# The two left-over rows of each expert: half of their gate and up products moved from TensorE to VectorE

## The chip, the cores and the metric

The kernel runs on one core of a Trainium2 chip. The metric is device time in microseconds (us) of one execution; the median of three runs before the change was 2638.13 us. A core has TensorE (PE in the profile; its weight loads are PEld), VectorE (DVE), ScalarE (ACT), GpSimd (POOL) and SyncE (SP, which here only issues transfers), and 16 DMA engines that move data between memory (HBM) and the on-chip SBUF. TensorE writes its sums into PSUM.

## The reference, cut to what matters

Two transformer blocks run one after the other on 512 tokens of width 1024. The change lies in the last stage, the mixture of experts of the second block. Each of 16 experts takes the 66 of 528 tokens that score best for it (2 x 528 / 16), and computes on them

```
hg = einsum('becd,edf->becf', xg, w_gate)      # 66 x 1024 by 1024 x 2048
hu = einsum('becd,edf->becf', xg, w_up)        # 66 x 1024 by 1024 x 2048
y  = einsum('becf,efd->becd', silu(hg) * hu, w_down)   # 66 x 2048 by 2048 x 1024
y  = y * top_aff[..., None]
```

and adds the rows to the tokens that they came from. All of it is float32. One expert's three matrices are 25.2 MB, and each is used for 66 rows only.

## The kernel before

**The expert stage** is the last 40% of the program. Tokens are the stationary operand and weights are streamed through TensorE. The array is used in four quarters of 32 columns: `four` issues four matmuls of 128x32 by 128x512, one for each quarter, which run side by side. 64 of the 66 rows fill two quarters, so one `four` multiplies them with 2 x 512 columns of weights. The two left-over rows (`LEFT` = 2) take a `four` of their own, in which each quarter holds the same two rows and takes another 512 columns.

**The order on TensorE** (`expert`). The gate and up products are made in two halves h of 1024 columns each. A half has 8 steps k over the 1024 inputs, and each step has three `four`s: gate, up (the 64 rows), and left-over. Both halves make 48 `four`s. `turn_hidden` transposes the products of the 64 rows and of the left-over rows back into stationary form, in the midst of the second half for h = 0 and within the down stage for h = 1. The down product is 24 `four`s: in four pieces (h, b) of 4 for the 64 rows and 2 for the left-over rows. That is 72 `four`s for an expert. `turn_x` transposes the next expert's gathered tokens before the last piece.

**The weights** come in 12 loads of 2 MB for each expert (0 to 3 gate and up of the first half, 4 to 7 of the second, 8 to 11 down), into a ring of 8 slots (`expert_ring_low`, `expert_ring_high`). SyncE issues them strictly in order (`pair_loads`, `load_read`): load n waits until the slot of load n - 8 has been read, which TensorE tells by the counts `w_used`, `left_summed` and `down_left_summed`.

**The other engines.** ScalarE takes the silu of the gate sums and copies transposed data. VectorE multiplies with the up sums, copies, scales the next tokens (`take_x`) and, once the down sums are complete, the output rows (`YM` for 64 rows in two halves, `YL` for the left-over ones). GpSimd gathers the tokens of the expert after the next (`gather`) and adds the output rows to memory (`scatter`), by indirect transfers. Before the stage, ScalarE writes the tokens' rows to memory in 12 transfers out of the four buffers `TMS`; GpSimd's second gather waits for all 12 (`rows_out`).

The two SyncE lines on which a step of the prediction rests:

```
                if j in (3, 7):
                    sp.wait_ge(S("left_summed"), pair * 16 + 8 * r + (4 if j == 3 else 8))
```

## Time and profile before

| | |
|---|---|
| median of 3 runs | 2638.13 us (2638.09 to 2641.3) |
| the profiled execution, its own time | 2637.16 us |
| its span, first to last instruction | 2635.4 us |
| PE, DVE, ACT, POOL busy over the span | 95%, 42%, 31%, 14% |
| mean granted TensorE clock | 0.978 of full speed |
| the expert stage's matmuls, L1135 | 9216 records, 509.7 + 504.8 us busy |
| the 192 loads of expert weights | 2048 KB each, median 11.4 us from issue to landing |

Each float32 matmul of the program leaves two records in the trace, so a `four` is eight. GB/s is what all transfers of the core moved. A wait is written as: who waited, for whom, how long in total.

### The profile page before, as it was taken

How to read it: one execution, taken by the hardware profiler on the slowest of the kernel's cores; microseconds unless marked ns; L12 is line 12 of the kernel's file. 1: busy time of each engine (PE TensorE's matmuls, PEld its weight loads, DVE VectorE, ACT ScalarE, POOL GpSimd, SP SyncE). 2: the span in 40 equal slices, each digit the busy share in tenths (PEclk: the TensorE clock that was granted, in tenths of full speed). 3: DMA queues.
4: the chain of work that ended last, by engine and by line, in shares of the span. 5: the costliest groups of instructions: out<-in, count | busy, mean ns of one | idle time of the engine just before them, and what ended most of it. 6: DMA issues, size and time to landing. Idle time of an engine off the chain costs nothing.

```text
span 2635.4 us, 42597 instructions
## 1 busy us (share of the span) xinstructions
PE 2514.9 (95%) x18335; PEld 1566.6 (59%) x18335; DVE 1097.4 (42%) x1506; ACT 821.0 (31%) x1361; POOL 374.0 (14%) x423
## 2 busy tenths in 40 slices
PE   8998899999989999999989979999999999999996
PEld 6755468887779898989889953333333333333332
DVE  4335456664538898987574541111111111111111
ACT  3255544443344545554545230000000000000001
POOL 0024012111102212123421200000000000000000
PEclk9999999999989999999989989999999999999998
DMA  5100068888845454646524549999999999999993
GB/s 206 71 32 1 32 239 289 290 281 283 276 158 192 150 196 136 201 145 217 146 96 162 212 153 408 400 398 401 395 400 398 396 395 395 395 397 401 396 406 120
DMA packets 129718, 676.36 MB, mean 257 GB/s; under 512 B 19300, under 2 KB 52068, under 8 KB 100228
## 3 DMA queue, kind: packets, MB, share of 16 engines
q1 hardware_dynamic: 56624, 554.81, 54.1%
q0 software_dynamic: 25632, 88.49, 10.0%
q10 hardware_dynamic: 47284, 30.42, 4.3%
q8 instruction: 145, 2.38, 0.4%
q14 instruction: 33, 0.27, 0.0%
HBM read 618.55 MB, written 55.12 MB: 256 GB/s over the span
## 4 chain that ended last, share of the span: by engine, by line
PE 79%; DVE 8%; DMA 6%; ACT 4%; issue 2%; POOL 1%; ACTq 0%; POOLq 0%; DVEq 0%
PE PS L1135 38%; PE PS L825 11%; PE PS L1007 4%; PE PS L771 3%; PE PS L767 3%; DMA arena<-w_proj 3%; PE PS L768 3%; PE PS L1012 2%; DMA ring<-ssd_sums 2%; ACT ring L1509 2%; PE PS L671 1%; PE PS L622 1%; PE PS L618 1%; PE PS L619 1%; PE PS L742 1%
## 5 line engine op out<-in xcount | busy, mean ns | idle before, releaser
L1135 PE MATMUL PS<-expert_ring_low,U 128*32 128x512 f32 x4608 | 509.7, 594 | 0.9 <-DVE U L2264 0.9
L1135 PE MATMUL PS<-expert_ring_high,U 128*32 128x512 f32 x4608 | 504.8, 592 | 0.0
L825 PE MATMUL PS<-XH,RINGF 128*128 128x264 f32 x2304 | 393.9, 289 | 1.2 <-ACT arena L1453 1.2
L1135 PEld LDWEIGHTS PS<-expert_ring_high,U 128*32 128x32 f32 x4608 | 148.0, 110 | 336.9 <-issue 335.9
L1135 PEld LDWEIGHTS PS<-expert_ring_low,U 128*32 128x32 f32 x4608 | 146.2, 110 | 332.8 <-issue 331.7
L825 PEld LDWEIGHTS PS<-XH,RINGF 128*128 128x128 f32 x2304 | 325.6, 190 | 9.1 <-issue 6.8
L825 PE MATMUL PS<-UH,RINGF 128*128 128x264 f32 x1152 | 234.8, 286 | 0.0
L2276 DVE TENSOR_TENSOR H<-H,PS 128x512 f32<-128x512 f32 x32 | 22.0, 688 | 439.3 <-PE PS L1135 423.8
L2016 DVE SCALAR_TENSOR_TENSOR H<-arena,par,H 128x528 f32<-128x528 f32 x240 | 187.1, 823 | 1.3
L825 PEld LDWEIGHTS PS<-UH,RINGF 128*128 128x128 f32 x1152 | 180.7, 191 | 0.0
L1712 ACT ACTIVATE H<-PS 128x512 f32<-128x512 f32 x32 | 19.1, 598 | 457.8 <-PE PS L1135 457.8
L2465 POOL DMA_INDIRECT residual_rows<-H,scatter_rows x16 | 25.1, 1572 | 930.8 <-DVE H L2290 930.8
L767 PE MATMUL PS<-UX,WF 128*128 128x512 f32 x352 | 138.5, 393 | 1.0 <-DVE UX L1758 1.0
L768 PE MATMUL PS<-UX,WF 128*128 128x512 f32 x352 | 137.1, 389 | 0.0
L1896 DVE TENSOR_TENSOR PREL<-arena,PS 128x1024 fp32r<-128x1024 f32 x66 | 80.5, 1220 | 119.6 <-ACT PS L1360 119.4
L2067 DVE SCALAR_TENSOR_TENSOR SQ<-arena,par,SQ 128x528 f32<-128x528 f32 x144 | 109.7, 766 | 6.4 <-ACT SQ L1441 3.7
L1360 ACT ACTIVATE PS<-arena 128x1024 fp32r<-128x1024 f32 x66 | 67.8, 1027 | 142.8 <-DMA arena<-w_proj 141.1
L2371 POOL TENSOR_TENSOR arena<-arena,ring 128x512 f32<-128x512 f32 (+1 forms) x32 | 60.2, 1886 | 318.4 <-ACT arena L1534 258.7
L1723 ACT ACTIVATE SQ<-PS 2x512 f32<-2x512 f32 x32 | 18.9, 591 | 260.6 <-PE PS L1135 260.2
L1509 ACT ACTIVATE ring<-ring 128x128 f32<-128x128 f32 (+1 forms) x320 | 89.3, 368 | 17.9 <-issue 12.0
L2282 DVE COPY U<-PS 128x256 f32<-128x256 f32 x32 | 13.6, 425 | 191.1 <-PE PS L1129 191.1
L1344 ACT ACTIVATE WF<-ring 128x1024 fp32r<-128x1024 f32 (+1 forms) x76 | 71.3, 940 | 59.8 <-PE PS L771 59.6
(350 smaller groups left out, 3695.6 us busy)
## 6 DMA issues: line engine op xcount, KB each, us to landing
expert_ring_low<-w_experts SPq DMA_DIRECT2D x96, 2048.0 KB, 11.4
expert_ring_high<-w_experts SPq DMA_DIRECT2D x96, 2048.0 KB, 11.4
arena<-w_proj POOLq DMA_DIRECT2D x72, 512.0 KB, 5.0
projection_low_parts<-PREL POOLq DMA_DIRECT2D x72, 512.0 KB, 5.0
ring<-w_proj SPq DMA_DIRECT2D x72, 512.0 KB, 3.7
RINGF<-projection_low_parts SPq DMA_DIRECT2D x72, 512.0 KB, 4.7
ring<-w_gu SPq DMA_DIRECT2D x11, 2048.0 KB, 9.3
ring<-ssd_sums ACTq DMA_DIRECT2D x32, 512.0 KB, 8.4
```

The lines of the kernel that those rows point to most:

```text
L767: nc.tensor.matmul(PS[:, bank, :], hi[:, k, :], src[:, 0, k0 + k, :], start=(start and k == 0), stop=False)
L768: nc.tensor.matmul(PS[:, bank, :], hi[:, k, :], src[:, 1, k0 + k, :], start=False, stop=False)
L771: last = nc.tensor.matmul(PS[:, bank, :], lo[:, k, :], src[:, 0, k0 + k, :], start=False, stop=(stop and k == n - 1))
L825: last = nc.tensor.matmul(PS[:, banks[i], 0:HT], w[:, k, :], x[:, k, lo:hi], start=start, stop=stop)
L1007: nc.tensor.matmul(PS[:, banks[i], 0:HT], wh[:, k, :], x(k)[:, lo:hi], start=(first and k == 0 and x is high), stop=False)
L1135: mm = nc.tensor.matmul(PS[QUAD * t:QUAD * t + QUAD, bank, :], stat(t), move(t), start=start, stop=stop)
L1344: A(split_high(p), raw(p), ACT.Copy).then_inc(S("weights_high"), 1)
L1360: A(pre_high_place(q), pre_raw(q), ACT.Copy).then_inc(S("pre_high"), 1)
L1509: ins = A(FR[i % 2][d][0:n, h, 0:n], FR[i % 2][d][0:n, h, 0:n], ACT.Exp, bias=FT[0:n, c, j:j + 1])
L1896: V_.tensor_tensor(PREL[:, q % STAGE, :], pre_raw(q), pre_high_place(q).bitcast(F32), SUB).then_inc(S("pre_low"), 1)
L2016: ins = V_.scalar_tensor_tensor(acc, CP[:, u % 3, j:j + T2], par[:, w0 + j:w0 + j + 1], acc, MUL, ADD)
L2067: V_.scalar_tensor_tensor(co, xp[:, k:k + T2], par[:, w0 + k:w0 + k + 1], co, MUL, ADD)\
```

## The change

VectorE now makes the left-over rows' gate and up products of the first half. For each step k and each of the two rows a it multiplies the 128x2048 weights of the step with the row's input (one value for each partition) and adds that to `LACC[:, a, :]` (`left_steps`): 16 operations for an expert. TensorE then sums `LACC` over the partitions with two `four`s whose stationary operand `LONE` is a column of ones, instead of the eight `four`s of before. `LACC` lies in the memory of `TMS`, so VectorE waits for all row writes (`rows_out`) before it fills `LONE` and takes the first tokens.

With it the order moves: the left-over rows of the second half come first (q = 0 is h = 1), those of the first half second; in the down stage the 64 rows' products run ahead of the left-over ones. Slots 0 to 3 of an expert are free only when VectorE has read them too (the count `accumulated`, which is also the renamed `conf_tap` of an earlier stage). The loops over experts on VectorE and SyncE are unrolled.

```diff
+        LACC = TMS.rearrange("p b n -> p (b n)").rearrange("p (a n) -> p a n", a=LEFT)
+        LONE = arena[:, 6600:6600 + LEFT * QUAD].rearrange("p (a n) -> p a n", a=LEFT)
...
                         four(3 * h, token, lambda t: w[:, t // 2, :], first, last, *(("gate_summed",) if last else ()))
-                        four(3 * h + 1, token, lambda t: w[:, 2 + t // 2, :], first, last, *(("up_summed",) if last else ()))
-                        four(3 * h + 2, lambda t: XG[:, k, 0:QUAD], lambda t: w[:, t, :], first, last, *done)
+                        used = ("w_used",) if h == 0 and k % 2 and not last else ()
+                        four(3 * h + 1, token, lambda t: w[:, 2 + t // 2, :], first, last, *(("up_summed",) if last else used))
+                        if h == 1:
+                            done = ("left_summed",) if last else ("w_used",) if k % 2 else ()
+                            four(5, lambda t: XG[:, k, 0:QUAD], lambda t: w[:, t, :], first, last, *done)
                         if h == 1 and k == 2:
                             turn_hidden(e, 0)
+                pe.wait_ge(S("accumulated"), ACCUMULATED + (e + 1) * DT * LEFT)
+                for a in range(LEFT):
+                    four(2, lambda t: LONE[:, a, :], lambda t: LACC[:, a, 512 * t:512 * t + 512], a == 0, a == LEFT - 1,
+                         *(("left_summed",) if a == LEFT - 1 else ()))
...
+                down_main(0, 0)
+                turn_hidden(e, 1)
+                turn_left(e, 0)
+                down_main(0, 1)
+                turn_left(e, 1)
+                down_main(1, 0)
+                if turn_next:
+                    turn_x(e + 1)
+                down_left(0, 0)
+                down_left(0, 1)
+                down_main(1, 1)
+                down_left(1, 0)
+                down_left(1, 1)
...
+            def left_steps(e, k):
+                if k == 0:
+                    dve.wait_ge(S("xg_ready"), e * 2 + 2)
+                    if e > 0:
+                        dve.wait_ge(S("left_summed"), e * 8)
+                if k % 2 == 0:
+                    expert_landed(dve, e // 2, 12 * (e % 2) + k // 2)
+                w = er(12 * (e % 2) + k // 2)[:, 2048 * (k % 2):2048 * (k % 2) + 2048]
+                for a in range(LEFT):
+                    if k == 0:
+                        ins = V_.tensor_scalar(LACC[:, a, :], w, XG[:, k, a:a + 1], None, MUL)
+                    else:
+                        dve.wait_ge(S("accumulated"), ACCUMULATED + e * DT * LEFT + LEFT * (k - 1) + a + 1)
+                        ins = V_.scalar_tensor_tensor(LACC[:, a, :], w, XG[:, k, a:a + 1], LACC[:, a, :], MUL, ADD)
+                    ins.then_inc(S("accumulated"), 1)
...
+            for b in range(TSTAGE):
+                dve.wait_ge(S(f"rows_out{b}"), 16 * len(range(b, 2 * NR, TSTAGE)))
+            link(V_.memset(LONE[:, :, :], 0.0))
+            for a in range(LEFT):
+                link(V_.memset(LONE[:, a, a:a + 1], 1.0))
             take_x(0)
...
+            for k in range(2):
+                left_steps(0, k)
+            for e in range(EXPERTS):
+                for k in range(2, 5):
+                    left_steps(e, k)
+                inner(e, 0)
+                for k in range(5, DT):
+                    left_steps(e, k)
+                inner(e, 1)
+                inner_left(e, 0)
+                inner_left(e, 1)
+                left_copy(e, 0)
+                left_copy(e, 1)
+                if e < EXPERTS - 1:
+                    take_x(e + 1)
+                    for k in range(2):
+                        left_steps(e + 1, k)
+                rows_done(e)
...
-                if j in (3, 7):
-                    sp.wait_ge(S("left_summed"), pair * 16 + 8 * r + (4 if j == 3 else 8))
+                if j < 4:
+                    sp.wait_ge(S("accumulated"), pair * 32 + (ACCUMULATED + 16 * r + 4 * (j + 1)))
+                if j == 3:
+                    sp.wait_ge(S("up_summed"), pair * 16 + 8 * r + 4)
+                elif j == 7:
+                    sp.wait_ge(S("left_summed"), pair * 16 + 8 * r + 4)
```

VectorE at the start of the stage, before: the clearing of a hidden buffer (`H`), then at once the two halves of `take_x(0)` (they wait for nothing but the transposed tokens, `x_turned`).

```order
L2259 MEMSET H 64x1024 [waits freed3,freed0]
L2264 TENSOR_TENSOR U<-PS,par 128x264 [waits x_turned]
L2264 TENSOR_TENSOR U<-PS,par 128x264
L2269 COPY small<-arena 128x1
L2270 COPY small<-arena 2x1
L2276 TENSOR_TENSOR H<-H,PS 128x512 [waits up_summed,sil_ready]
```

The same place after the change, up to the first expert's `inner(0, 0)` (L2324). The row writes now stand ahead of `take_x(0)` (L2297), and ten long operations ahead of `inner`.

```order
L2292 MEMSET H 64x1024 [waits freed3,freed0]
L2359 MEMSET arena 128x64 [waits rows_out2,rows_out3,rows_out1,rows_out0]
L2361 MEMSET arena 128x1 [waits dve_chain] x2
L2297 TENSOR_TENSOR U<-PS,par 128x264 [waits x_turned,dve_chain]
L2297 TENSOR_TENSOR U<-PS,par 128x264
L2312 TENSOR_SCALAR arena<-expert_ring_low,U 128x2048 [waits expert_ring0,xg_ready]
L2312 TENSOR_SCALAR arena<-expert_ring_low,U 128x2048
L2315 SCALAR_TENSOR_TENSOR arena<-expert_ring_low,U,arena 128x2048 [waits accumulated] x2
L2315 SCALAR_TENSOR_TENSOR arena<-expert_ring_low,U,arena 128x2048 [waits accumulated,expert_ring1]
L2315 SCALAR_TENSOR_TENSOR arena<-expert_ring_low,U,arena 128x2048 [waits accumulated] x3
L2315 SCALAR_TENSOR_TENSOR arena<-expert_ring_low,U,arena 128x2048 [waits accumulated,expert_ring2]
L2324 TENSOR_TENSOR H<-H,PS 128x512 [waits up_summed,sil_ready]
```

SyncE, after the change: the loads into the slots that the second expert's gate and up weights leave. The first four wait for VectorE's count as well; SyncE issues in order, so the loads behind them (`w_used` of the second half) wait too. Before, the same rows read `w_used` and, for the fourth, `left_summed`.

```order
L2614 DMA expert_ring_high<-w_experts 128x4096 [waits w_used,accumulated]
L2614 DMA expert_ring_low<-w_experts 128x4096 [waits w_used,accumulated]
L2614 DMA expert_ring_high<-w_experts 128x4096 [waits w_used,accumulated]
L2614 DMA expert_ring_high<-w_experts 128x4096 [waits up_summed,accumulated]
L2614 DMA expert_ring_low<-w_experts 128x4096 [waits w_used] x3
L2614 DMA expert_ring_high<-w_experts 128x4096 [waits left_summed]
```

## Rows read from the trace of the kernel before

**Rows 1.** The page: TensorE's share, and GB/s in 40 slices of 65.9 us.

```profile
PE 2514.9 (95%) x18335; PEld 1566.6 (59%) x18335; DVE 1097.4 (42%) x1506; ACT 821.0 (31%) x1361; POOL 374.0 (14%) x423
...
GB/s 206 71 32 1 32 239 289 290 281 283 276 158 192 150 196 136 201 145 217 146 96 162 212 153 408 400 398 401 395 400 398 396 395 395 395 397 401 396 406 120
```

**Rows 2.** The chain that ended last, around the stage's end: start, us, what.

```profile
2597.27 14.85 PE PS L1135 x136
2612.12 0.04 DVEq L2289
```

**Rows 3.** Timeline of PE inside an expert: start, us, instruction, count of records.

```profile
1650.21 10.48 PE L1135 MATMUL PS<-expert_ring_high,U 128*32 128x512 f32 x96
1660.51 7.91 PE L1135 MATMUL PS<-expert_ring_low,U 128*32 128x512 f32 x72
1668.35 0.66 PE L1125 MATMUL PS<-consts_sb,H 128*128 128x128 f32 x4
...
1669.37 7.93 PE L1135 MATMUL PS<-expert_ring_low,U 128*32 128x512 f32 x72
```

**Rows 4.** Timeline of SP: issues of loads 8, 92, 93 and 189 (two rows merge more).

```profile
1580.49 10.63 SPq L2536 DMA_DIRECT2D expert_ring_low<-w_experts  x3
...
2034.93 0.33 SPq L2536 DMA_DIRECT2D expert_ring_high<-w_experts  x1
2040.09 0.33 SPq L2536 DMA_DIRECT2D expert_ring_low<-w_experts  x1
...
2559.18 0.33 SPq L2536 DMA_DIRECT2D expert_ring_low<-w_experts  x1
```

**Rows 5.** Windows: us, busy of each engine, clock, DMA share, GB/s.

```profile
1840.00:1904.90 64.90, 64.90 (x604) 20.70 (x600) 7.43 (x14) 5.34 (x9) 3.91 (x4) 1.00 1.00 397
1888.00:1904.00 16.00, 16.00 (x156) 5.15 (x152) 3.54 (x6) 1.77 (x3) 1.57 (x1) 1.00 0.97 371
1904.00:1920.00 16.00, 16.00 (x152) 4.81 (x148) 0.59 (x3) 0.60 (x1) 2.34 (x2) 1.00 1.01 347
1920.00:1936.00 16.00, 16.00 (x152) 5.30 (x148) 1.48 (x3) 1.19 (x2) 0.00 (x0) 1.00 1.01 427
```

**Rows 6.** Expert loads, issue to landing: whole span, then 1700 to 2560 us.

```profile
DMA to landing us min/median/max: 7.6/11.4/24.4
...
DMA to landing us min/median/max: 7.8/11.3/14.9
```

**Rows 7.** Waits of the SP queue, 1645 to 2575 us: total, times, longest.

```profile
SPq L2536 <- PE PS L1135: 835.2, 172, 6.0
```

**Rows 8.** Groups of DVE by form: busy, mean ns of one, idle before.

```profile
L2016 DVE SCALAR_TENSOR_TENSOR H<-arena,par,H 128x528 f32<-128x528 f32 x240 | 187.1, 823 | 1.3
L2067 DVE SCALAR_TENSOR_TENSOR SQ<-arena,par,SQ 128x528 f32<-128x528 f32 x144 | 109.7, 766 | 6.4 <-ACT SQ L1441 3.7
...
L1884 DVE TENSOR_TENSOR RINGF<-ring,WF 128x1024 fp32r<-128x1024 f32 x44 | 53.8, 1223 | 12.4 <-ACT WF L1344 12.3
L2034 DVE TENSOR_TENSOR RINGL<-ring,WH 128x1024 fp32r<-128x1024 f32 x32 | 46.0, 1451 | 63.7 <-ACT WH L1566 57.5 <-DMA H<-residual 6.2
...
L2295 DVE TENSOR_SCALAR U<-SQ,small 2x1024 f32<-2x1024 f32 x16 | 11.9, 742 | 0.6
...
L2308 DVE SCALAR_TENSOR_TENSOR expert_ring_low<-expert_ring_low,small,arena 128x1024 f32<-128x1024 f32 x4 | 5.1, 1285 | 0.1
```

**Rows 9.** Timelines of DVE, PE, ACT and POOL at the stage's start.

```profile
1572.93 0.70 DVE L2264 TENSOR_TENSOR U<-PS,par 128x264 f32<-128x264 f32 x2
...
1573.68 8.80 PE L1135 MATMUL PS<-expert_ring_low,U 128*32 128x512 f32 x68 [0.93 <-DVE U L2264]
...
1571.84 0.29 ACTq L1702 DMA_DIRECT2D residual_rows<-arena  x1
...
1583.76 0.97 POOL L2459 DMA_INDIRECT U<-normed_rows,gather_rows  x1 [15.67 <-DMA residual_rows<-arena]
```

More of the change, by code:

```diff
@@ new lines, in down_main @@
+                def down_main(h, b):
+                    w = down_weights(h, b)
+                    pe.wait_ge(S("hgm_ready"), e * 2 + h + 1)
+                    for j in range(4):
+                        first, last = h == 0 and b == 0 and j == 0, h == 1 and b == 1 and j == 3
+                        four(6, lambda t: HGM[:, h, j, 64 * b + QUAD * (t % 2):64 * b + QUAD * (t % 2) + QUAD],
+                             lambda t: w[:, j, t // 2, :], first, last, *(("down_summed",) if last else ()))
@@ new lines, in down_left @@
+                def down_left(h, b):
+                    w = down_weights(h, b)
+                    pe.wait_ge(S("hgl_ready"), e * 2 + 2 - h)
+                    for j in range(0, 4, 2):
+                        first, last = h == 0 and b == 0 and j == 0, h == 1 and b == 1 and j == 2
+                        four(7, lambda t: HGL[:, h, j + t // 2, QUAD * b:QUAD * b + QUAD], lambda t: w[:, j + t // 2, t % 2, :],
+                             first, last, *(("down_left_summed",) if last else ("w_used",) if j == 2 else ()))
@@ L1450, in conf_gate @@
                 if u >= 3:
-                    act.wait_ge(S("conf_tap"), TAPS_TO[u - 3])
+                    act.wait_ge(S("accumulated"), TAPS_TO[u - 3])
                 b = bank(("ca", u))
@@ L1632, in _ @@
                 scan_copy(m)
-            act.wait_ge(S("conf_tap"), DT * CONF_TAPS)
+            act.wait_ge(S("accumulated"), DT * CONF_TAPS)
             gates_stored(act)
@@ L1712, in expert @@
                     A(SIL[:, h, :], PS[:, 3 * h, :], ACT.Silu).then_inc(S("sil_ready"), 1)
-                    act.wait_ge(S("left_summed"), e * 8 + 4 * h + 4)
-                    if not (first and h == 0):
-                        act.wait_ge(S("hid_left_ready"), e * 2 + h + 1)
-                    A(SILL[64:P, :], PS[0:64, 3 * h + 2, :], ACT.Silu).then_inc(S("sil_left_ready"), 1)
+                    if h == 1:
+                        for q in range(2):
+                            act.wait_ge(S("left_summed"), e * 8 + 4 * q + 4)
+                            if not (first and q == 0):
+                                act.wait_ge(S("hid_left_ready"), e * 2 + q + 1)
+                            A(SILL[64:P, :], PS[0:64, 3 * (1 - q) + 2, :], ACT.Silu).then_inc(S("sil_left_ready"), 1)
                     act.wait_ge(S("hid_turned"), e * 2 + h + 1)
@@ new lines, in inner, with inner_left @@
+            def inner(e, h):
+                dve.wait_ge(S("sil_ready"), e * 2 + h + 1)
+                dve.wait_ge(S("up_summed"), e * 8 + 4 * h + 4)
+                if e > 0:
+                    dve.wait_ge(S("hid_turned"), e * 2 + h - 1)
+                V_.tensor_tensor(HID[:, h, :], SIL[:, h, :], PS[:, 3 * h + 1, :], MUL).then_inc(S("hid_ready"), 1)
+            def inner_left(e, q):
+                h = 1 - q
+                dve.wait_ge(S("sil_left_ready"), e * 2 + q + 1)
+                if e > 0:
+                    dve.wait_ge(S("hid_left_turned"), e * 2 + q - 1)
+                V_.tensor_tensor(HIDL[64:P, h, :], SILL[64:P, :], PS[64:P, 3 * h + 2, :], MUL).then_inc(S("hid_left_ready"), 1)
@@ new lines, in left_copy, with rows_done @@
+            def left_copy(e, q):
+                h = 1 - q
+                dve.wait_ge(S("hid_left_turned"), e * 2 + q + 1)
+                V_.tensor_copy(HGL[:, h, :, :], PS[:, 3 * h + 2, :].rearrange("p (j n) -> p j n", j=4)[:, :, 64:P])\
+                    .then_inc(S("hgl_ready"), 1)
+            def rows_done(e):
+                V_.tensor_copy(AFS[:, 0:1], AFT[:, e:e + 1, 0]).then_inc(S("aff_copied"), 1)
+                V_.tensor_copy(AFS[0:LEFT, 1:2], AFT[0:LEFT, e:e + 1, 1]).then_inc(S("aff_copied"), 1)
@@ L2286, in expert @@
                 dve.wait_ge(S("aff_copied"), e * 2 + 2)
                 dve.wait_ge(S("down_summed"), e * 4 + 4)
-                if not first:
+                if e > 0:
                     dve.wait_ge(S("y_added"), e * 32)
@@ L2296, in expert @@
                 dve.wait_ge(S("yl_ready"), e + 1)
-            take_x(0)
-            expert(0, first=True)
-            with dve.Fori(1, EXPERTS - 1) as e:
-                expert(e)
-            expert(EXPERTS - 1, take_next=False)
+            for b in range(TSTAGE):
[3 more added lines that the diff above has]
+                link(V_.memset(LONE[:, a, a:a + 1], 1.0))
+            take_x(0)
+            for k in range(2):
[16 more added lines that the diff above has]
+                rows_done(e)
             dve.wait_ge(S("gains_in"), 16)
@@ L2571, in _ @@
             sp.dma_start(FG, inp["final_row"][0].partition_broadcast(P)).then_inc(S("gains_in"), 16)
-            with sp.Fori(1, EXPERTS // 2 - 1) as pair:
+            for pair in range(1, EXPERTS // 2 - 1):
                 pair_loads(pair, 24)
```

56 lines of the change are left out of this document (14 added, 42 removed).

## Prediction

> **What bounds the kernel now.** I read the page first: TensorE is busy 95% of the span, and from slice 25 on, where the expert stage lies, the transfers run at 395 to 408 GB/s in every slice but the last [rows 1]. So two things may bound the stage, and the question is which one is free to follow when the other gets shorter. The chain that ended last runs over L1135, the experts' matmuls, until 2612.12 us [rows 2], and never over a load of weights: TensorE bounds the stage today. The timeline gives the price of a `four`: 96 records, 12 `four`s, from 1650.21 to 1660.51, so 0.858 us [rows 3]. The issues of loads that lie whole experts apart give the period of an expert: 2034.93 - 1580.49 over seven, and 2559.18 - 2040.09 over eight, both 64.9 us [rows 4]. 72 `four`s are 61.8 of it; a stop for transposes is 1.0 (1668.35 to 1669.37), and there are three.
>
> Then the other side. In a full stretch with no indirect transfers the core moved 427 GB/s, and the sixteen engines were busy all the time (share 1.01). In the 16 us with the scatter and the gather it moved 347, just before them 371 at a share of 0.97, and 397 over the whole period [rows 5]. A load took at least 7.8 us from issue to landing in the steady stage, against 7.6 for one on its own, and 11.3 in the middle [rows 6]: the queue of loads almost drains once in an expert, and not more. SyncE waits for TensorE nearly all the time, 835.2 us over 172 loads [rows 7], so the loads are started by TensorE's pace; but what they have to spare is small. I estimate it in two ways. What moves in a period is 397 x 64.9 = 25.8 MB, which at 427 takes 60.3 us; the scatter's stretch loses 16 x (427 - 347) / 427 = 3.0 on top: **63.3 us** for an expert if loads are always waiting. The stretch ahead of it lost 16 x (427 - 371) / 427 = 2.1, which is the whole slack. The other bound is **64.9**: the load that lands last is set by the slowest of 16 engines, and the shortest landing was 0.2 us off an idle queue's only once, so the slowest engine may have had no slack at all. The Trainium skill ("DMA: Bandwidth & Descriptors", Specifications) gives 435 GB/s as the ceiling of the fabric; the trace's 427 agrees, so no queueing trick makes the 25.2 MB of an expert come in less than about 58 us by that page, and the change takes no byte away.
>
> **The change, part by part.**
> TensorE: eight `four`s go, two come: -6 x 0.858 = -5.1 us for an expert. The same transposes stand in four stops instead of three, +0.4 by the half of a stop [rows 3]. TensorE alone would need 64.9 - 5.1 + 0.4 = 60.2 us. That is below both bounds of the loads, so the loads become the pace: an expert takes P, between 63.3 and 64.9; I take the middle, 64.1.
>
> VectorE: 14 operations of the multiply-and-add over 128x2048. The trace has this operation at 528 columns in 766 ns and at 1024 in 1285 [rows 8]; the slope is 1.046 ns a column, so 2048 take 2.35 us. The two k = 0 products are TENSOR_SCALAR; 1024 columns on two partitions took 742 [rows 8], so at most 1.48 each and, if some 200 ns of it are fixed, 1.28. Together 14 x 2.35 + 2 x 1.28 = 35.5 us, beside 7.4 that VectorE does today in a period [rows 5]: 43 of 64. That is hidden if it comes in time at three places. First, `inner(e, 0)` stands behind k = 2 to 4, and TensorE waits for it at `turn_hidden`. In steady pace `rows_done` of the expert before ends about 4 us into the expert (the ScalarE copies and three small operations behind the last down sums); 6 x 2.35 + 0.75 later is 19; TensorE comes there after 16 + 9 `four`s, at 21.4. Second, the last step ends at 4 + 12 x 2.35 + 0.75 = 33; TensorE comes to its `accumulated` wait after 40 `four`s and a stop, at 35, and at the loads' pace 3 to 4 us later. Third, the slots: 0 to 3 are released at about 4, 14, 24 and 33 us instead of 5, 10, 15 and 21, and 4 to 6, which TensorE has read by 30, come with slot 3, since SyncE issues in order. That bunches the issues: few in the first half of an expert, five at 33, four in the last ten. It starves the loads only if the queue runs dry; with the loads as the pace about five are outstanding when the slow stretch begins, 24 us of work, so it doesn't, once the stage has settled. Price: nothing in steady pace, and in the first expert the sum below. The queue that is bunched up is used by nobody but the loads; the gathers and scatters go by GpSimd's queue and are early by most of an expert.
>
> The start: `take_x(0)` ran at 1572.93 and the first expert began at 1573.68. It now stands behind the writes of the rows. The last write was issued at 1571.84, and GpSimd, which waits for the same writes, went on at 1583.76 [rows 9]. With the three memsets (0.2 us each, as small operations) and `take_x` the first expert starts at about 1584.5: **+10.8 us**, and nothing covers it, because VectorE's count also holds the slots.
>
> The sum, for the end of the matmuls. In the first expert VectorE starts when TensorE starts: slots free at 7.3, 16.7, 26.8 (with `inner` in between) and 36.2 us, so load 11 is issued at 36.6 and lands 7.6 later [rows 6], at 44.2. With it slots 4 to 6 are free, and from here loads are always waiting. 180 loads are left, 15 experts' worth: 15 x 64.1 = 961.5. Behind the last landing TensorE still has to do what it can't do faster than the loads came: from load 4 of the last expert on (24 + 2 + 24 `four`s less the seven loads' 4.9 us each, with the stops) 11.1 us. 1584.5 + 44.2 + 961.5 + 11.1 = 2601.3, against 2612.1 [rows 2]: **-10.8 us**. Today's kernel ends 33 us behind its last landing, since TensorE is the slower one; this lead, 22 us, is what pays for the later start, and P does the rest: 15 x 0.8 = 12. What follows behind the matmuls is as before. From the profiled execution's 2637.16 that gives 2626.4; the median of the runs is 1.0 above it: **2627**.
>
> **The rivals.**
> (a) The loads have no slack, P = 64.9: the sum ends 12 us later, +1.2: no change. For it: landing times that hardly reach the idle value [rows 6]. Against: share and GB/s do fall in each period [rows 5].
> (b) VectorE becomes the pace, and the kernel is slower. Its steps are bunched between `rows_done` and TensorE's `accumulated` wait. At P = 64.1 there is 39 - 33 = 6 us to spare over 12 operations, so it decides from 2.8 us an operation on. For it: the same subtraction of 128x1024 took 1223 ns at L1884 and 1451 at L2034, 19% more, and L2016 took 823 where L2067 took 766 [rows 8]; 2.35 x 1.19 is just 2.8. The Trainium skill ("SBUF — State Buffer", Who interferes with whom) says that a VectorE operation with two SBUF inputs and a GpSimd one that reads SBUF shut each other out for a whole instruction; the new operation has two. GpSimd is busy 3.9 us in a period [rows 5], so even full exclusion leaves 2 of the 6 us. At 2.9 us the last step ends at 40; then 2 `four`s, the down stage's 24 and its stops bring an expert back to 64.8; the lead is gone and the start and the first expert (+6) are paid: about +14, 2652. At 3.1 it would be 2690.
> (c) TensorE stays the pace, 60.2 us: P would need loads at over 427 GB/s with the scatters. 15 x 3.9 = 58 below the forecast, 2570. Only if the 427 is no ceiling; no row of the stage shows more.
> (d) TensorE, which now waits some 4 us in an expert, is granted the lower of its clock levels for part of the time. In the stage before it the clock stayed at 1.00 [rows 5], in the start it was lower after a pause. Each lost us counts only beyond the 4 of slack; I give it a few us at worst, within (a).
>
> **How the numbers follow.** Loads as the pace with P from 63.3 to 64.4: -23 to -5, 2615 to 2633: 0.55. (a), (d) and P around 64.9: within 5 us of before: 0.20. (b), or loads that come worse than today because they are bunched (P over 65.2 is +6): 0.23. (c) 0.02. A difference under 0.2%, 5.3 us, is what I count as no change. The likeliest own range is 2615 to 2633; with (a) and the milder part of (b) it is 2613 to 2652. Faster 0.57, same 0.20, slower 0.23.
>
> **What would show it.** The first L1142 matmul at about 1584, behind the memsets at L2359. L2315 at 2.3 to 2.4 us. Issues of loads in a pattern of one, one, one, five. GB/s at 400 to 408 over a period with a share of 1.00 to the end, and the last load landing some 11 us ahead of the last matmul instead of 33. TensorE waiting once an expert, for a load of the ring, about 4 us; if its waits name VectorE (L2315) instead, (b) is right. A period of 64.9 with a landing-bound TensorE is (a). The forecast is wrong above all if the length of L2315 or P is: one us of P is 15 us of the result.

## The result, and the profile after

The changed kernel takes 2607.3 us in the median (2603.48 to 2608.65), the kernel before 2639.7 on the same chip: a ratio of 0.9873, with a 95% interval of 0.9856 to 0.989. That is 1.3% faster, 32 us by the medians where the forecast was 11, and below the range of 2615 to 2633.

The page of the changed kernel, its first part and GB/s in 40 slices of 65.1 us, answers to [rows 1]:

```profile
PE 2444.6 (94%) x17567; PEld 1539.2 (59%) x17567; DVE 1641.8 (63%) x1765; ACT 820.6 (31%) x1361; POOL 411.2 (16%) x423
...
GB/s 204 77 32 1 33 239 293 287 284 271 257 200 182 152 189 146 199 150 204 172 99 107 188 178 248 414 410 413 414 415 411 412 411 413 413 407 412 410 417 220
```

From slice 26 to 39 the transfers run at 407 to 417 GB/s, where the kernel before has 395 to 408. Slice 25 (1563 to 1628 us) shows 248: there the loads are held up at the stage's start. The timelines at the stage's start answer to [rows 9]: start, length, engine, instruction, and what ended the idle time before it.

```profile
1570.79 0.29 ACTq L1733 DMA_DIRECT2D residual_rows<-arena  x1
...
1582.71 0.11 DVE L2359 MEMSET arena<- 128x64 f32 x1 [10.76 <-DMA residual_rows<-arena]
...
1583.94 12.35 PE L1142 MATMUL PS<-expert_ring_low,U 128*32 128x512 f32 x96 [12.22 <-DVE U L2297]
```

VectorE waits 10.8 us for the rows' last write, and the first expert's matmuls come 10.3 us later than in [rows 9]. VectorE's new work, by form (busy, mean ns of one, idle before), answers to [rows 8]:

```profile
L2315 DVE SCALAR_TENSOR_TENSOR arena<-expert_ring_low,U,arena 128x2048 f32<-128x2048 f32 x112 | 256.1, 2347 | 0.5
L2312 DVE TENSOR_SCALAR arena<-expert_ring_low,U 128x2048 f32<-128x2048 f32 x16 | 19.9, 1284 | 16.0 <-DMA expert_ring_low<-w_experts 15.9
```

The period of an expert is best read from the transposes of the next expert's rows (L1120), once in each. Timeline of PE: those of experts 1 to 4 and 14, and the stage's last matmuls.

```profile
1634.87 0.71 PE L1120 MATMUL PS<-consts_sb,U 66*128 66x66 f32 x8
...
1694.91 0.71 PE L1120 MATMUL PS<-consts_sb,U 66*128 66x66 f32 x8
...
1754.95 0.71 PE L1120 MATMUL PS<-consts_sb,U 66*128 66x66 f32 x8
...
1818.21 0.71 PE L1120 MATMUL PS<-consts_sb,U 66*128 66x66 f32 x8
...
2447.49 0.71 PE L1120 MATMUL PS<-consts_sb,U 66*128 66x66 f32 x8
...
2575.05 7.05 PE L1142 MATMUL PS<-expert_ring_high,U 128*32 128x512 f32 x64
```

Two experts take 60.04 us each, then an expert takes (2447.49 - 1754.95) / 11 = 62.96. Two paces, then: TensorE alone at 60.04 while the loads that were already in the ring last, and the loads behind it. The waits name it. PE in 1590 to 2580 us, then the SP queue in 1645 to 2560, which answers to [rows 7] (total, times, longest), then all expert loads of 1700 to 2540 from issue to landing, as [rows 6], and the window of twelve experts, as [rows 5]:

```profile
PE PS L1142 <- DMA expert_ring_low<-w_experts: 22.6, 16, 3.2
PE PS L1142 <- DMA expert_ring_high<-w_experts: 5.8, 6, 2.3
```

```profile
SPq L2614 <- PE PS L1142: 391.1, 81, 16.1
SPq L2614 <- DVE arena L2315: 361.9, 45, 9.2
SPq L2644 <- PE PS L1142: 88.4, 29, 3.1
```

```profile
DMA to landing us min/median/max: 20.6/28.0/33.5
```

```profile
1728.11:2484.85 756.74, 728.35 (x6628) 226.41 (x6632) 501.03 (x363) 64.10 (x108) 78.12 (x36) 1.00 1.01 412
```

No matmul waits for VectorE; every wait is for a load. TensorE is busy 728 of 757 us and idle the rest, 2.4 us an expert; its mean clock rounds to 1.00. A load stands in the queue for 28 us instead of 11: loads are always waiting, and the DMA engines never drain.

### The profile page after: what moved, and what is told of

Read it like the earlier page. It is cut to its first block, busy times and chain, and to the rows that moved or that the text cites. A ratio compares the mean times of both kernels' runs of the same rounds, so it can differ in the third digit from the quotient of the medians.

```text
span 2605.3 us, 40945 instructions
## 1 busy us (share of the span) xinstructions
PE 2444.6 (94%) x17567; PEld 1539.2 (59%) x17567; DVE 1641.8 (63%) x1765; ACT 820.6 (31%) x1361; POOL 411.2 (16%) x423
## 4 chain that ended last, share of the span: by engine, by line
PE 66%; DMA 19%; DVE 7%; ACT 4%; issue 2%; POOL 1%; ACTq 0%; POOLq 0%; DVEq 0%; SPq 0%
PE PS L1142 23%; DMA expert_ring_low<-w_experts 12%; PE PS L828 12%; PE PS L1010 4%; PE PS L774 3%; PE PS L770 3%; PE PS L771 3%; DMA arena<-w_proj 3%; PE PS L745 2%; PE PS L1015 2%; DMA ring<-ssd_sums 2%; ACT ring L1540 2%; PE PS L674 1%; PE PS L621 1%; PE PS L622 1%
## 5 line engine op out<-in xcount | busy, mean ns | idle before, releaser
L1142 PE MATMUL PS<-expert_ring_low,U 128*32 128x512 f32 x4096 | 464.4, 597 | 34.8 <-DMA expert_ring_low<-w_experts 22.6
L1142 PE MATMUL PS<-expert_ring_high,U 128*32 128x512 f32 x4096 | 457.4, 594 | 5.8 <-DMA expert_ring_high<-w_experts 5.8
L1142 PEld LDWEIGHTS PS<-expert_ring_low,U 128*32 128x32 f32 x4096 | 126.7, 110 | 327.2 <-issue 276.0
L1142 PEld LDWEIGHTS PS<-expert_ring_high,U 128*32 128x32 f32 x4096 | 131.0, 110 | 308.7 <-issue 295.5
L2315 DVE SCALAR_TENSOR_TENSOR arena<-expert_ring_low,U,arena 128x2048 f32<-128x2048 f32 x112 | 256.1, 2347 | 0.5
L2315 DVE SCALAR_TENSOR_TENSOR arena<-expert_ring_high,U,arena 128x2048 f32<-128x2048 f32 x112 | 256.1, 2348 | 0.0
L2543 POOL DMA_INDIRECT residual_rows<-H,scatter_rows x16 | 25.9, 1616 | 867.8 <-DVE H L2349 867.8
L1743 ACT ACTIVATE H<-PS 128x512 f32<-128x512 f32 x32 | 19.1, 597 | 366.7 <-PE PS L1142 366.7
```

The costliest lines, as they stand in the source:

```text
L1142: mm = nc.tensor.matmul(PS[QUAD * t:QUAD * t + QUAD, bank, :], stat(t), move(t), start=start, stop=stop)
L2315: ins = V_.scalar_tensor_tensor(LACC[:, a, :], w, XG[:, k, a:a + 1], LACC[:, a, :], MUL, ADD)
```

## The experiments

One thing has to be known to read the runs. What comes ahead of the expert stage is the same code in all, but its length differs between executions: the last write of a row (L1733 here) was issued at 1570.79 us in the changed kernel, at 1562.35 in one kernel below and at 1580.26 in another. So beside the ratio to the kernel before stands a length taken inside one trace: from the issue of the last row write to the end of the stage's last matmul. It is taken from one trace for each kernel, so 1 or 2 us of it are no finding by themselves. The period is that of the steady part, from two of the transposes' rows; the count of experts between them is in brackets. Each ratio is to the kernel before as it ran beside that kernel, on the same chip (medians from 2634.6 to 2639.7 us), so rows are compared by ratio or by length, and their medians only roughly.

| kernel | ratio [95%] | median us | write to last matmul us | period us |
|---|---|---|---|---|
| before | 1 | 2639.7 | 1041.0 | 64.90 |
| after | 0.9873 [0.9856, 0.989] | 2607.3 | 1011.3 | 62.96 (11) |
| take_first | 0.9896 [0.9881, 0.9911] | 2611.0 | 1009.8 | 62.94 (11) |
| split | 0.9854 [0.9839, 0.9869] | 2598.4 | 1000.2 | 62.97 (11) |
| no_scatter | 0.9839 [0.9825, 0.9852] | 2594.1 | 995.8 | 61.73 (9) |
| left_out | 0.9796 [0.9783, 0.981] | 2582.9 | 990.2 | 62.80 (10) |
| first_plain | 0.9855 [0.9835, 0.9876] | 2598.4 | 1002.1 | 62.86 (10) |
| no_gather | 0.9775 [0.9754, 0.9797] | 2576.4 | 980.1 | 60.39 (14) |
| dve_more | 0.9895 [0.987, 0.992] | 2608.4 | 1011.7 | 62.93 (11) |
| dve_most | 0.9908 [0.9882, 0.9934] | 2610.7 | 1014.8 | 63.16 (11) |
| two_out | 0.9929 [0.9906, 0.9951] | 2616.3 | 1015.9 | 63.68 (11) |
| three_out | 0.988 [0.9858, 0.9902] | 2603.5 | 1009.7 | 62.84 (11) |
| order_only | 1.0021 [1.0005, 1.0036] | 2641.5 | 1046.0 | 65.19 (14) |
| late_start | 1.0049 [1.0032, 1.0065] | 2648.5 | 1053.1 | 64.90 (14) |

### What held the start: take_first, split, first_plain, late_start

```diff
+            take_x(0)
             for b in range(TSTAGE):
                 dve.wait_ge(S(f"rows_out{b}"), 16 * len(range(b, 2 * NR, TSTAGE)))
             ...
-            take_x(0)
```

> The changed kernel, but take_x(0) stands ahead of the wait for the rows' writes, so TensorE's first expert matmul comes some 10 us earlier (at about 1574 instead of 1584), while VectorE's steps start when they did. Theory (the loads are the pace, and VectorE's count of steps holds the first slots): no gain, 2607 us, within 2 of the changed kernel. Rival (the delayed start of TensorE is what costs): about 10 us faster, 2597.

The stage got 1.5 us shorter, not 10: 1009.8 against 1011.3; the ratio's interval overlaps with that of the changed kernel. Timeline of PE, its first matmul and its next stop:

```profile
1579.82 10.51 PE L1142 MATMUL PS<-expert_ring_low,U 128*32 128x512 f32 x96 [0.93 <-DVE U L2297]
...
1611.29 1.12 PE L1128 MATMUL PS<-consts_sb,H 128*128 128x128 f32 x4 [9.80 <-DVE H L2324]
```

The matmuls start 1.8 us behind the last row write (1577.98) instead of 13, and then TensorE stands 9.8 us before the hidden rows' transposes, since VectorE's product L2324 comes behind the steps of k = 2 to 4. VectorE's steps hold the start, as the theory had it: the first slot is released 19.1 us behind the last row write against 20.2 in the changed kernel (load 8 at 1597.09 and at 1590.95). Beside the slots they hold TensorE itself in the first expert. In this trace the granted clock is also 0.50 from 1606 to 1616, from 4.5 us into that stop on, and the 24 records behind the stop's transposes take 4.68 us instead of 2.78; so 2 us of what an earlier TensorE might gain are lost to the clock here.

```diff
-        LACC = TMS.rearrange("p b n -> p (b n)").rearrange("p (a n) -> p a n", a=LEFT)
+        LACC = [arena[:, 2112:11216].rearrange("p (b n) -> p b n", b=2)[:, :, 0:1024],
+                arena[:, 3136:5184].rearrange("p (b n) -> p b n", b=2)]
 ...
+            take_x(0)
+            for a in range(LEFT):
+                for b in ((0,), (1, 2))[a]:
+                    dve.wait_ge(S(f"rows_out{b}"), 16 * len(range(b, 2 * NR, TSTAGE)))
+                for k in range(3):
+                    left_steps(0, k, (a,))
             ...
```

> The changed kernel, with the two accumulators laid where columns come free sooner: row 0's in row buffer 0 and in free columns, row 1's in buffers 1 and 2. VectorE does three steps of row 0 while the last rows are still being written, then three of row 1. By the trace of the changed kernel its steps then start at about 1574 instead of 1583.9, with at most 1 us lost at 1580.7; the slots of the ring are released some 6 to 9 us earlier in the first expert. Theory (a stream of loads as the pace, which only the first expert's slots delay): 6 to 9 us faster, 2598 to 2601. Rival (the loads have a slack somewhere that eats it, or the split pattern makes each step slower): 2605 to 2612.

Timeline of DVE in this kernel, whose last row write was issued at 1567.84:

```profile
1569.71 1.29 DVE L2313 TENSOR_SCALAR arena<-expert_ring_low,U 128x2048 f32<-128x2048 f32 x1
1571.04 4.81 DVE L2317 SCALAR_TENSOR_TENSOR arena<-expert_ring_low,U,arena 128x2048 f32<-128x2048 f32 x2
1575.76 1.28 DVE L2313 TENSOR_SCALAR arena<-expert_ring_low,U 128x2048 f32<-128x2048 f32 x1
```

The steps start 1.9 us behind that write instead of 13, and the second row's follow without a gap. The stage is 11.1 us shorter than the changed kernel's and the period the same; the median is 2598, inside what was expected. By the ratios to the kernel before (0.9854 and 0.9873) the gain over the changed kernel is only 5 us, with intervals that overlap a little. The earlier start is shown by the traces; what it is worth, 5 or 11 us, is not settled. This is the fastest kernel here that computes everything, level with the next one.

```diff
-                        if h == 1:
-                            done = ("left_summed",) if last else ("w_used",) if k % 2 else ()
-                            four(5, lambda t: XG[:, k, 0:QUAD], lambda t: w[:, t, :], first, last, *done)
+                        if h == 1 or e == 0:
+                            done = ("left_summed",) if last else ("w_used",) if k % 2 else ()
+                            four(3 * h + 2, lambda t: XG[:, k, 0:QUAD], lambda t: w[:, t, :], first, last, *done)
                         ...
```

The rest of the edit (dots) lets VectorE's steps, its wait for the row writes and SyncE's waits for its count begin with expert 1.

> The changed kernel, but in expert 0 TensorE does the first-half products of the left-over rows as the kernel before did, and VectorE's accumulation begins with expert 1. Nothing then waits for the rows' writes at the start, and the first slots are released at TensorE's pace. Theory (stream of loads as the pace, at 62.9 us an expert; only what load 11's landing gains counts): load 11 was issued 21 us behind the first matmul in the kernel before, so at about 1595, and lands at about 1603 instead of 1627.4: 24 us faster, 2583 us; 2580 to 2588. Rival (TensorE's longer first expert is not made up for, since TensorE is no faster than the loads): it would start expert 1 at 1638.6, 10 us earlier than in the changed kernel, and gain 10 us only, 2597.

The theory fell and the rival held: 9.2 us shorter than the changed kernel, not 24. Timeline of SP in this trace, where everything stands 9.5 us later than in the changed kernel's:

```profile
1590.49 10.63 SPq L2614 DMA_DIRECT2D expert_ring_low<-w_experts  x3
1605.94 5.48 SPq L2614 DMA_DIRECT2D expert_ring_high<-w_experts  x2
1616.96 0.33 SPq L2614 DMA_DIRECT2D expert_ring_low<-w_experts  x1
1622.11 5.48 SPq L2614 DMA_DIRECT2D expert_ring_high<-w_experts  x2
1641.94 7.19 SPq L2614 DMA_DIRECT2D expert_ring_low<-w_experts  x3
```

The first slot is indeed released 8 us behind the first matmul (1582.10), by TensorE. But the ninth of these loads needs the slot in which expert 0's first block of down weights lies, and SyncE issues nothing from 1627.6 to 1641.9, until TensorE is through with it. So the stream of loads has two gates in its first round, VectorE's count and TensorE's own length; opening the first moves the wait to the second.

```diff
+            for b in range(TSTAGE):
+                dve.wait_ge(S(f"rows_out{b}"), 16 * len(range(b, 2 * NR, TSTAGE)))
             take_x(0)
             expert(0, first=True)
```

> The kernel before with VectorE's wait for the rows' writes ahead of take_x(0), nothing else. Theory (in the kernel before TensorE is the pace from its first matmul on): +10 to +11 us, 2648 to 2651. Rival (the loads' slots or something later hides it): within 4 us of before.

+12.0 us in the stage, with the period unchanged at 64.90; the ratio of 1.0049 is +13, the expectation 10 to 11. In the kernel before TensorE is the pace from its first matmul on, and the wait costs its full length, and 1.4 us more. The first matmul comes 12.45 us behind the last row write instead of 1.84, so 10.6 later; the rest is in the first 144 records, in late_start and then in the kernel before:

```profile
1590.98 18.39 PE L1135 MATMUL PS<-expert_ring_low,U 128*32 128x512 f32 x144 [11.53 <-DVE U L2264]
```

```profile
1573.68 16.96 PE L1135 MATMUL PS<-expert_ring_low,U 128*32 128x512 f32 x144 [0.93 <-DVE U L2264]
```

Behind the stop of 11.5 us the granted clock is 0.67 in the first 10 us (1590 to 1600), against 0.83 in the kernel before (1573 to 1583).

### What sets the period: left_out, no_scatter, no_gather, two_out, three_out

This kernel leaves out, of the kernel before, the left-over rows' first-half products of k = 0 to 6.

```diff
                         ...
-                        four(3 * h + 2, lambda t: XG[:, k, 0:QUAD], lambda t: w[:, t, :], first, last, *done)
+                        if h == 1 or last:
+                            four(3 * h + 2, lambda t: XG[:, k, 0:QUAD], lambda t: w[:, t, :], first or h == 0, last, *done)
```

> The kernel before, in which TensorE leaves out the first-half products of the left-over rows for k = 0 to 6 and nothing does them (the left-over rows' output is incomplete). TensorE is then shorter than in the changed kernel, VectorE reads no weights, and nothing is late at the start. Theory (the pace is the loads with their scatter, 62.9 us, and VectorE's reading costs nothing in it): load 11 lands at about 1600, 15 x 62.9 later is 2543, and about 11 us behind it the matmuls end: 2582 us. Rival 1 (VectorE's reading of the weights slows the loads): P below 62.4, so under 2575. Rival 2 (bunched issues help the loads, and TensorE's even ones don't): P of 64 or more, 2598 and up.

In lines not shown, the up products of the 64 rows now tell SyncE that a slot is read (`w_used`). The result is 2582.9 us, as the theory had it. Its transposes of experts 4 and 14:

```profile
1807.27 0.71 PE L1117 MATMUL PS<-consts_sb,U 66*128 66x66 f32 x8
...
2435.30 0.71 PE L1117 MATMUL PS<-consts_sb,U 66*128 66x66 f32 x8
```

Until the first of them TensorE took 58.9 us an expert (1689.49 to 1748.38 to 1807.27); then the loads caught up with it and it is 62.80. With VectorE out of it and TensorE 1.1 us shorter than in the changed kernel, the period stays within 0.2 us. So the pace of 62.9 is the loads', in the order of the kernel before as in the new one, and VectorE's reading of the same weights costs them 0.2 at most.

```diff
                 ...
-                if e > 0:
-                    pool.wait_ge(S("y_added"), 32 * e)
-                G_.indirect_dma_start(h_half_rows, rows_of(SI, P, e), YM, None, compute_op=ALU.add).then_inc(S("y_added"), 16)
                 pool.wait_ge(S("yl_ready"), e + 1)
-                ...
+                if e == EXPERTS - 1:
+                    G_.indirect_dma_start(h_half_rows, rows_of(SI, P, e), YM, None, compute_op=ALU.add).then_inc(S("y_added"), 16)
+                    ...
```

> The changed kernel without the scatters of 15 of the 16 experts (only the last expert's rows are added, so the output lacks the others); gathers, matmuls and VectorE's work stay. Theory (62.9 us an expert is 58.6 of undisturbed loads and about 4 that the scatter takes): the loads would need about 59.5, TensorE alone 60.2, so an expert takes 60.2 to 60.8 and the kernel 2607 - 15 x 2.4 = 2571, give or take 5. Rival (the period is set by something else than the scatters, VectorE's steps or TensorE's waits): within 8 us of the changed kernel.

The period fell by 1.2 us, not by the 2.2 to 2.8 of the theory, which charged the scatters too much; the rival, no effect beyond 8 us, is out as well, with a stage 15.5 us shorter. The windows of this trace around a gather (us, busy of PE, PEld, DVE, ACT, POOL, clock, DMA share, GB/s) say what takes the rest:

```profile
1834.00:1842.00 8.00, 8.00 (x80) 2.47 (x76) 7.93 (x6) 0.00 (x0) 2.39 (x1) 1.00 1.01 428
1842.00:1848.00 6.00, 6.00 (x60) 1.82 (x56) 6.00 (x4) 0.60 (x1) 0.00 (x0) 1.00 1.02 320
1848.00:1856.00 8.00, 8.00 (x76) 2.52 (x72) 8.00 (x5) 0.60 (x1) 0.00 (x0) 1.00 1.01 417
```

In the 6 us of the gather all transfers together move 320 GB/s, at a full DMA share. Hence the next kernel, with the first gather alone; every expert computes with expert 0's rows.

```diff
-                if e < EXPERTS - 1:
-                    gather(e + 1)
                 scatter(e)
                 ...
```

> The changed kernel with the first expert's gather alone (every expert computes with expert 0's rows, so the output is not the reference's); the scatters stay. In the trace without scatters the packets of the loads took 0.75 to 0.83 us instead of 0.55 in the 6 us of a gather, and an expert still 61.7 us. Theory (the gather takes 2.4 to 2.8 us of the loads, the scatter 1.2): the loads need 60.1 to 60.5, TensorE 60.2 to 60.8: 15 x 2.3 = 34 faster, 2568 to 2578. Rival (what slows the loads there lies in the load stream itself, at the ring's turn for example): within 8 us of 2607.

The stage is 31 us shorter than the changed kernel's, and 2576 is what the theory had (2568 to 2578). The transposes of experts 1 and 8:

```profile
1633.92 0.72 PE L1120 MATMUL PS<-consts_sb,U 66*128 66x66 f32 x8
...
2054.20 0.71 PE L1120 MATMUL PS<-consts_sb,U 66*128 66x66 f32 x8
```

(2054.20 - 1633.92) / 7 = 60.04: TensorE's own pace, for half of the stage; over all it is 60.39. The second half is the one to set against the steady 62.96, since the first lives on loads that were already in the ring:

```profile
2479.36 0.71 PE L1120 MATMUL PS<-consts_sb,U 66*128 66x66 f32 x8
```

(2479.36 - 2054.20) / 7 = 60.74, with the DMA engines never idle (share 1.01 from 2054 to 2480). So the gather, 66 rows of 4 KB, costs the loads some 62.96 - 60.74 = 2.2 us an expert, a little less than the theory's 2.4 to 2.8, and the two scatters 1.2; by the lengths of the stages, over 15 experts, it is 2.1 and 1.0.

```diff
                 for i in range(n):
                     load_read(pair, i)
+                    m = ERING + 24 * pair + i - 2
+                    sp.wait_ge(S(f"expert_ring{m % ERING}"), 16 * (m // ERING + 1))
```

> The changed kernel, in which SyncE waits behind each issue of a load in the ring until the load two before it has landed on all 16 engines, so at most two or three loads are outstanding instead of up to six. Two loads are 9.8 us of transfers against a landing time of 7.6 for one on an idle queue, so undisturbed stretches stay full. Theory (the deep queue is why the scatter and gather cost 3.9 us an expert instead of the 5.5 to 6 seen in the kernel before, where the shortest landing was 7.6: an engine that is behind holds up the others only when the queue is shallow): 64.5 to 65 us an expert, 2630 to 2640. Rival (the cost is in the indirect transfers themselves): within 5 us of the changed kernel's 2607.

> As two_out, with one load more outstanding. Theory: between the two, 63.2 to 64.3 us an expert, 2611 to 2627. Rival: within 5 us of 2607.

 (with - 3 in the place of - 2)

Loads from issue to landing, 1700 to 2540 us, in two_out and then in three_out:

```profile
DMA to landing us min/median/max: 9.7/10.0/14.0
```

```profile
DMA to landing us min/median/max: 14.4/15.0/19.2
```

The queue became as shallow as it was meant to, and the periods are 63.68 and 62.84. three_out isn't slower at all (1009.7 against 1011.3), so from some three loads on the depth counts for nothing; two_out pays 0.7 us an expert, less than half of what the theory wanted, and 4.6 us in the whole stage. The theory is out, and the rival is the nearer one: most of the cost is in the indirect transfers themselves. A stream with a median of 10.0 us to landing, less than the 11.3 of [rows 6], keeps 63.7.

### VectorE's length, and the order: dve_more, dve_most, order_only

```diff
                     ins.then_inc(S("accumulated"), 1)
+                    if k > 0:
+                        at = 6700 + 400 * ((2 * k + a) % 3)
+                        V_.memset(arena[:, at:at + 400], 0.0)
```

> The changed kernel with a memset of 128x160 behind each of VectorE's 14 multiply-and-adds of an expert, about 0.2 us each, 2.7 us an expert. In the trace of the changed kernel VectorE stands idle 5.5 us ahead of its second inner product and some more elsewhere, and landings take 14 us and more from issue in most of the stage. Theory (VectorE's length counts only in the first expert, where its count holds the slots): +2 to +4 us, 2609 to 2612. Rival (VectorE is near the pace, since slots 0 to 3 are released by its count): 15 x 1 us or more, 2620 and up.

 (with 160 in the place of 400)

> As dve_more with 400 columns, about 0.43 us each, 6 us an expert: an operation and its share of the memset take 2.75 us, where the forecast put the threshold at 2.8. Theory (idle time of 5.5 us ahead of the second inner product, and a queue deep enough but in the last experts): +6 in the first expert, and from nothing to 1 us in each of the others, 2613 to 2628. Rival 1 (VectorE is the pace from the first added ns on): 6 us in each expert, 2690. Rival 2 (no effect outside the first expert): 2613.

 (the kernel shown, with 400)

Groups of DVE by form in dve_most, 1600 to 2560 us, then its transposes of experts 1, 2, 3:

```profile
L2315 DVE SCALAR_TENSOR_TENSOR arena<-expert_ring_low,U,arena 128x2048 f32<-128x2048 f32 x107 | 242.1, 2262 | 0.5
L2319 DVE MEMSET arena<- 128x400 f32 x218 | 85.5, 392 | 7.1
```

```profile
1636.78 0.71 PE L1120 MATMUL PS<-consts_sb,U 66*128 66x66 f32 x8
...
1697.38 0.72 PE L1120 MATMUL PS<-consts_sb,U 66*128 66x66 f32 x8
...
1758.00 0.71 PE L1120 MATMUL PS<-consts_sb,U 66*128 66x66 f32 x8
```

A step costs 2262 + 392 = 2.65 us there against 2.35, 4.3 us more in the 14 steps of an expert. Where TensorE is the pace, in the first experts, this shows: 60.6 instead of 60.04. Where the loads are, hardly: 63.16 against 62.96. The stage is 3.5 us longer in all, and 0.4 with dve_more: less than either was expected to cost in the first expert alone (6 and 2 to 4). Rival 1, 6 us in each expert, is out. The threshold itself was not reached.

order_only has the new order and the written-out loops, and all products on TensorE:

```diff
                         ...
-                        if h == 1:
-                            done = ("left_summed",) if last else ("w_used",) if k % 2 else ()
-                            four(5, lambda t: XG[:, k, 0:QUAD], lambda t: w[:, t, :], first, last, *done)
+                        done = ("left_summed",) if last else ("w_used",) if k % 2 else ()
+                        four(3 * h + 2, lambda t: XG[:, k, 0:QUAD], lambda t: w[:, t, :], first, last, *done)
                         ...
```

> The changed kernel's order (left-over halves turned late, down products in the new order, loops written out), but TensorE does all products of the left-over rows and VectorE none of the accumulation; no wait for the rows' writes at the start. Theory (TensorE is the pace as in the kernel before, one more stop of 0.4 us an expert, nothing else): 2638 to 2648. Rival (the new order takes waits off TensorE and is part of the gain): 2625 to 2632.

65.19 us an expert, 0.29 more than before; 14 of them are 4 of the 5.0 us by which the stage got longer. The order brings nothing by itself; it costs the fourth stop.

## Why the prediction was wrong

The direction and the mechanism were right, and the sum fails in one term. By its steps:

- **Start, +10.8.** Measured 10.3 by the first matmul, 11.3 counted from the last row write; late_start, which has this wait and nothing else, pays 12.0, of which 1.4 are the lower clock behind the stop. Right.
- **TensorE alone, 60.2.** 60.04 in the first experts. Right; so are the eight `four`s less and two more, and the 0.4 for a fourth stop (0.29 in order_only).
- **VectorE, 2.35 and 1.28 us.** 2347 and 1284 ns. Right, and so is that it hides: rival (b) had its threshold at 2.8 us, and 2.65 cost 0.2 us an expert at the loads' pace.
- **"The loads become the pace."** Right: no wait for VectorE, waits for the ring only, about 2.4 us an expert where I said about 4.
- **"An expert takes P, between 63.3 and 64.9; I take the middle, 64.1."** Here it failed. P is 62.96, below the lower bound. 15 experts at 1.1 us are 17 of the 19 us by which the matmuls ended ahead of the forecast (2582.10 against 2601.3); load 11, issued at 1618.70 and not at 1621.1, gives most of the rest.

The term went wrong in two places. The upper bound rested on the slowest of 16 engines: "the slowest engine may have had no slack at all", read from landings of 7.8 us. left_out refutes it: in the order of the kernel before, with a shorter TensorE, an expert takes 62.80. So does two_out. With landings of 9.7 to 14.0, about as tight as in [rows 6], the loads keep 63.7, so in the kernel before they had at least 1.2 us to spare, and with one more load outstanding 2. A landing time near an idle queue's says that the queue is empty when the load is issued. That is what a stream with time to spare looks like; it can't be turned into a sign that it has none. The middle between the bounds brought in 0.8 of the 1.1 us (64.1 against 63.3).

The lower bound itself was 0.3 too high. It charged the whole deficit of one slow stretch, 347 against 427 GB/s [rows 5], as a loss that stays. That stretch was a bad one. The same 16 us of the expert before it lost 16 x (427 - 365) / 427 = 2.3 us, not 3.0:

```profile
1840.00:1856.00 16.00, 16.00 (x152) 4.81 (x148) 0.69 (x1) 0.97 (x2) 1.51 (x2) 1.00 1.01 365
```

With 2.3 the working of the prediction closes, too: 60.3 + 2.3 + 2.1 is 64.7 of the 64.9, where 3.0 makes it 65.4.

And part of the loss went with the change. In the 24 us behind the issue of the large scatter, on the mean of eleven experts, the kernel before moved 369 GB/s, the changed one 389, two_out 385 and three_out 389; in the rest of an expert they moved 414, 426, 420 and 424. A queue of two loads thus costs some 0.2 us in the slow stretch (385 against 389) and 0.6 outside it (420 against 426). That doesn't account for the 369 of the kernel before, and no run here tells apart what does. The bound treated as certain what the change itself was to alter.

Of the rivals, (a) is refuted by left_out and two_out, (b) by dve_most as far as it went. (d) did happen, and was as small as it was put. The granted clock is at the lower level, 1.2 GHz, in two stretches of 3.4 us, which the mean of the long window hides:

```profile
2229.40:2232.80 3.40, 2.88 (x16) 0.78 (x20) 3.40 (x3) 0.00 (x0) 0.00 (x0) 0.50 1.01 429
2475.20:2478.60 3.40, 3.40 (x24) 0.86 (x19) 3.40 (x3) 0.00 (x0) 0.00 (x0) 0.50 1.01 355
```

The first begins within a stop of 3.2 us in which TensorE waited for a load, the second just behind one of 2.3. Each stretch takes at most 1.7 us from TensorE, which waits for loads anyway.

(c), TensorE as the pace, 2570, is what no_gather comes near (2576), with work taken away. It was held to be possible "only if the 427 is no ceiling", and nothing here shows more for long: the best of the windows of 16 us that were read, of any kernel, have 428, and the mean of no_gather's second half is 421. What keeps TensorE 2.9 us above its own pace is neither the ceiling nor the 25.2 MB of loads, 58.9 us at 427, by itself: it is the 3.4 us that gather and scatters take from them on top. Together these are 62.3 of the 62.96; the last 0.6 is not assigned.

What is open: why the gather costs over three times its bytes (2.2 us, where 0.27 MB are 0.6 us at 427). Its packets, or the loads' own slowed beside them, were not told apart by an experiment.

## What to carry to other kernels

When a second resource takes over the pace, its time is not between its own estimate and the old period: the old period says only that it was no slower than that. Read the landing time against the queue's depth before calling a stream tight, and take the lower bound as the likeliest unless a row shows the resource itself waiting for nothing. And price every other user of that resource: here a gather of 1% of the bytes costs 3.5% of the period. Check such a price on more than one stretch of the trace; the one taken here was the worse of two neighbours.

A wait at the start costs its full length only if it holds up the engine or the queue that sets the pace from then on (late_start against take_first). The first round of a ring has a gate for each reader of a slot, and opening one shows the next (first_plain).

## What was not expected of the hardware

VectorE's steps were never held up by GpSimd: all 224 multiply-and-adds took 2342 to 2355 ns. GpSimd's issues of indirect transfers were held up instead. Groups of POOL in 1700 to 2540 us, in the kernel before and then in the changed one:

```profile
L2467 POOL DMA_INDIRECT residual_rows<-U,gather_rows x13 | 17.6, 1351 | 30.9 <-DVE U L2295 30.9
L2459 POOL DMA_INDIRECT U<-normed_rows,gather_rows x13 | 12.9, 996 | 4.0 <-issue 4.0
```

```profile
L2545 POOL DMA_INDIRECT residual_rows<-U,gather_rows x14 | 46.0, 3283 | 22.4 <-DVE U L2354 21.4 <-issue 0.9
L2537 POOL DMA_INDIRECT U<-normed_rows,gather_rows x13 | 20.9, 1605 | 4.0 <-issue 4.0
```

The issue of the small scatter went from 1351 to 3283 ns and that of the gather from 996 to 1605. In left_out and in order_only, where VectorE doesn't accumulate, they are 1350 and 995, with loads waiting in the queue in the first and the new order in the second; so it is VectorE's steps that lengthen them. The prediction had weighed the rule of the Trainium skill ("SBUF — State Buffer", Who interferes with whom) that a VectorE operation with two SBUF inputs and a GpSimd one that reads SBUF shut each other out; here it shows on GpSimd's side alone. The same section of the Trainium skill says that a DMA stalled by VectorE is one of the software queue, whose descriptors GpSimd is late to write; the lengths agree with it. Nobody waits for it here, as the gather is early by most of an expert.

The rest is told above: the gather lets all transfers together fall from 428 to 320 GB/s for 6 us, with the DMA share at 1.02, and the part of the program that no kernel here changes differs by up to 18 us between executions (1562.35 to 1580.26 at its last row write).
